# Two MoE blocks on one core: small broadcasts later at the opening, router products ahead of the norm's root, selections in fewer instructions

## The reference, cut to what matters

```python
h2 = rms_norm(x, norm2_gain[l]) * (1.0 + sc2) + sh2          # block 1
logits = (xf @ w_router + b_router)                           # 256 x 32
top_vals, top_idx = lax.top_k(logits, TOP_K)                  # top 4, softmax over them
# each of 32 experts: 1024 -> 2048, clipped SwiGLU, 1024 -> 1024
h2 = rms_norm_2(x, norm_ffn_g[l])                             # block 2
g_logits = hf @ w_rg + b_rg; e_logits = hf @ w_re + b_re      # 4 groups, 8 experts in each
# top 1 group, top 2 in it; 32 experts 1024 -> 2 x 256 -> 1024
```

## Time and profile before

| | us |
|---|---|
| median of 3 runs | 1674.42 (1673.65 to 1681.63) |
| profiled execution, whole time | 1677.89 |
| its span in the trace | 1676.10 |
| PE busy | 1496.8 (89%) |
| DVE busy | 645.1 (38%) |
| ACT busy | 326.2 (19%) |
| POOL busy | 11.9 (1%) |

### The profile page before, as it was taken

The page is one execution under the profiler, slowest core; times in us unless marked ns, Lnnn a source line. Parts: engine busy times, 40 slices in busy tenths (PEclk is TensorE's granted clock), DMA queues, the critical chain, the costliest instruction groups (busy, mean ns, idle before and its releaser), DMA issues.

```text
span 1676.1 us, 21107 instructions
## 1 busy us (share of the span) xinstructions
PE 1496.8 (89%) x8666; PEld 768.8 (46%) x8666; DVE 645.1 (38%) x1086; ACT 326.2 (19%) x374; POOL 11.9 (1%) x24
## 2 busy tenths in 40 slices
PE   3998999999989999898999989899889899997677
PEld 1776976333323333232333323233249898654343
DVE  2878576132313222231322223132257586431211
ACT  2444332110101011010101101010033454111110
POOL 1000000000000000000000000000000000000000
PEclk9999999999999999999999999999989899998989
DMA  9956255799999999999999999999955337599997
GB/s 349 355 226 252 101 179 214 323 428 430 427 429 427 430 427 430 427 430 427 429 428 429 428 429 428 429 428 429 425 195 200 105 147 279 239 415 422 422 422 296
DMA packets 73236, 592.31 MB, mean 353 GB/s; under 512 B 4946, under 2 KB 6056, under 8 KB 33252
## 3 DMA queue, kind: packets, MB, share of 16 engines
q1 hardware_dynamic: 71856, 588.27, 85.0%
q0 software_dynamic: 1088, 2.74, 0.7%
q10 hardware_dynamic: 244, 0.61, 0.1%
HBM read 590.55 MB, written 1.05 MB: 353 GB/s over the span
## 4 chain that ended last, share of the span: by engine, by line
DMA 50%; PE 37%; DVE 8%; ACT 2%; issue 2%; SPq 0%; DVEq 0%; ACTq 0%
DMA ring<-in_w_up 41%; PE PS L488 33%; DMA ring<-in_w_up_e 4%; DMA ring<-in_w_down_e 3%; PE PS L626 2%; DMA arena<-in_w_in 2%; DVE ring_r L330 1%; PE PS L648 1%; ACT ring_r L325 1%; DVE arena_r L330 0%; DVE arena L1758 0%; DVE arena L1999 0%; ACT arena L983 0%; PE PS L1198 0%; PE PS L578 0%
## 5 line engine op out<-in xcount | busy, mean ns | idle before, releaser
L488 PE MATMUL PS<-ring,arena 128*64 128x512 f32 x3072 | 686.4, 597 | 65.0 <-DMA ring<-in_w_up 57.6
L488 PEld LDWEIGHTS PS<-ring,arena 128*64 128x64 f32 x3072 | 212.6, 137 | 501.6 <-issue 385.5
L488 PE MATMUL PS<-arena 64*128 64x512 f32 (+12 forms) x1176 | 217.4, 448 | 13.3 <-DVE arena L2050 4.5
L703 DVE TENSOR_SCALAR arena<-PS 128x512 f32<-128x512 f32 x32 | 22.1, 692 | 514.4 <-PE PS L488 514.4
L488 PE MATMUL PS<-ring_r 128*128 128x256 f32 (+1 forms) x608 | 187.8, 313 | 0.0
L488 PEld LDWEIGHTS PS<-arena 128*64 128x64 f32 (+6 forms) x1176 | 105.6, 170 | 122.9 <-issue 107.9
L468 ACT ACTIVATE arena<-arena 128x512 f32<-128x512 f32 x32 | 20.2, 630 | 725.8 <-DVE arena L703 725.8
L488 PE MATMUL PS<-hT_r,ring_r 128*128 128x256 f32 x800 | 153.0, 288 | 1.7 <-DVE ring_r L330 1.7
L330 DVE TENSOR_TENSOR ring_r<-ring,ring_r 128x2048 fp32r<-128x2048 f32 x51 | 116.4, 2291 | 52.0 <-ACT ring_r L325 51.1
L488 PEld LDWEIGHTS PS<-hT_r,ring_r 128*128 128x128 f32 x800 | 129.1, 195 | 4.4 <-DVE ring_r L330 2.1
L325 ACT ACTIVATE ring_r<-ring 128x2048 fp32r<-128x2048 f32 x51 | 97.2, 1910 | 124.1 <-PE PS L488 113.5
(11 more groups left out here) (365 smaller groups left out, 1008.6 us busy)
## 6 DMA issues: line engine op xcount, KB each, us to landing
ring<-in_w_up SPq DMA_DIRECT2D x128, 2048.0 KB, 25.2
ring<-in_w_down SPq DMA_DIRECT2D x64, 2048.0 KB, 21.7
ring<-in_w_in SPq DMA_DIRECT2D x17, 2048.0 KB, 8.9
ring<-in_w_down_e SPq DMA_DIRECT2D x16, 2048.0 KB, 19.6
ring<-in_w_up_e SPq DMA_DIRECT2D x15, 2048.0 KB, 19.4
ring<-in_w_gate_e SPq DMA_DIRECT2D x14, 2048.0 KB, 20.9
ring<-in_w_ada SPq DMA_DIRECT2D x12, 2048.0 KB, 14.5
ring<-in_w_out SPq DMA_DIRECT2D x4, 2048.0 KB, 7.8
```

The lines of the kernel that those rows point to most:

```text
L488: return nc.tensor.matmul(o, w, m, start=first, stop=last)
L703: V.tensor_scalar(glu.rearrange("p (kk b q) -> p kk b q", kk=4, b=2), hu[:, :, :, :, 0], 7.0, None, ALU.min)\
```

## The change: what it does

**Opening.** In 0 is loaded as two halves; `consts` is cut: its first 136 columns stay on ACT's queue, the other 960 go on SP's queue behind in 0. The smalls wait on POOL until in 0 has landed, and behind a subtraction that POOL now does (the lower part of piece 0, DVE's before). `first_tokens` starts when the first four k-slices of `hT_up` are written. The n1 transposes stand ahead of ada 2 on PE.

**Routers.** n2: h without root and shift is transposed half by half and multiplied; the shift's share of the logits is a product of its own (added to `b_r1`); logits are scaled by `rs` afterwards. n4: the gain is multiplied before the root, and the logits scaled afterwards. Fewer `keep_warm` products stand between the steps. ACT does all of hT's copies in n2, and the first tile's in n4.

**Selections.** One DVE instruction with a broadcast operand replaces two (block 1) or eight (block 2); the first gather waits for the first selection alone. `moe2_gather` signals each half, ACT copies each half.

```diff
@@ consts and first unit
-_const("inv_freq", ...)            # last
+_const("inv_freq", ...)            # behind "ident"
+NFIRST = CONST["inv_freq"][0] + CONST["inv_freq"][1]
+                if u == IN0:
+                    w = t["w_in"][0, :, IN_COLS[0][0]:IN_COLS[0][0] + 512].rearrange("(k p) n -> p k n", p=P)
+                    for half, name in ((0, "first_half"), (1, f"loaded{SLOT_OF[u]}")):
+                        sp.dma_start(slots[SLOT_OF[u]][:, 2048 * half:2048 * (half + 1)].rearrange("p (k n) -> p k n", n=512),
+                                     w[:, 4 * half:4 * half + 4, :]).then_inc(S(name), 16)
+                    sp.dma_start(consts[:, NFIRST:], t["consts"][:, NFIRST:]).then_inc(S("consts"), 16)
@@ POOL
+            pool.wait_ge(S("w_upper"), 1)
+            nc.gpsimd.tensor_tensor(PIECES[0][3], PIECES[0][2], upper(0), ALU.subtract).then_inc(S("first_lower"), 1)
+            wait(pool, loaded(IN0))
             small_load(sm("hg_gain"), bc(t["hg_norm_gain"][0]), "smalls")
@@ PE, opening
-            ada(2)
             transpose_h(pe, "n1")
+            ada(2)
             ada(3)
...
-            pe.wait_ge(S("hT_V"), 1)
-            pe.wait_ge(S("hT_A"), 1)
             first_tokens()
@@ PE, router 1
-            keep_warm(7, 7)
-            transpose_h(pe, "n2")
-            router_mm(pe, "n2", sm("w_r1").rearrange("p (k n) -> p k n", k=KD), NE)
-            keep_warm(4, 7)
+            transpose_half(pe, 0)
+            pe.wait_ge(S("gain_free"), 1)
+            for k in range(KD):
+                last = mm(PS[:, 6, 480:512], sm("shiftT")[:, k:k + 1].broadcast_to([P, P]), w_r1[:, k, :], k == 0, k == KD - 1)
+            last.then_inc(S("logits"), 1)
+            keep_warm(1, 7)
+            transpose_half(pe, 1)
+            pe.wait_ge(S("hT_A"), 2)
+            for i in range(TT):
+                router_mm(w_r1, NE, i, range(4))
+            for i in range(TT):
+                pe.wait_ge(S("hT_A"), 3 + i)
+                last = router_mm(w_r1, NE, i, range(4, KD))
+            last.then_inc(S("logits"), 1)
+            keep_warm(2, 7)
             positions_mm(pe, "n2")
@@ DVE, logits of both routers
+            def logits(n, name, ne):
+                v.wait_ge(S("logits"), n)
+                for i in range(TT):
+                    last = STT(out=LG[:, i, 0:ne], in0=PS[:, 4 + i, 0:ne], scalar=sm("rs")[:, i:i + 1], in1=sm(name),
+                               op0=ALU.mult, op1=ALU.add)
+                L(last)
@@ DVE, selection of block 2
-        def moe2_select(X, e0, iota):
-            for i in range(TT):
-                for j in range(4):
-                    c = i * P + j * CAP2
-                    col = bass.ds(e0 + j, 1)
-                    V.tensor_scalar(selS2[:, c:c + CAP2], iota, SL[:, i, col], None, ALU.is_equal)
-                    last = V.tensor_scalar(selW2[:, c:c + CAP2], iota, SL[:, i, col], G[:, i, col], ALU.is_equal, ALU.mult)
+        def moe2_select(v, X, g, e0, iota):
+            cols_ = bass.ds(e0, 4)
+            for i in range(TT):
+                tile = selS2[:, i * P:(i + 1) * P].rearrange("p (j s) -> p j s", j=4)
+                last = V.tensor_tensor(tile, bc_mid(iota, 4), bc_last(SL[:, i, cols_], CAP2), ALU.is_equal)
+            last.then_inc(S(f"{X}_sel"), 1)
+            v.wait_ge(S(f"{X}_sel"), 2 * g + 1)
+            for i in range(TT):
+                s_, w_ = (a[:, i * P:(i + 1) * P].rearrange("p (j s) -> p j s", j=4) for a in (selS2, selW2))
+                last = V.tensor_tensor(w_, s_, bc_last(G[:, i, cols_], CAP2), ALU.mult)
             last.then_inc(S(f"{X}_sel"), 1)
```

More of the change, by code:

```diff
@@ L448, in rms_sums @@
                             .then_inc(S("squares"), 1)
+                if i == 0 and between:
+                    between()
             act.wait_ge(S("mean_square"), k)
             nc.scalar.sqrt(sm("rs"), sm("ss")[:, 0:2]).then_inc(S("rms"), 1)
[L452 to L455, removed]
         def moe1_act_gather(act, X, g):
@@ L472, in moe2_act_gather @@
         def moe2_act_gather(act, X, g):
-            act.wait_ge(S(f"{X}_gath_done"), g + 1)
-            nc.scalar.activation(xg2, PS[:, 0:2, :], ACT.Copy).then_inc(S(f"{X}_xg"), 1)
+            for b in range(2):
+                act.wait_ge(S(f"{X}_gath_done"), 2 * g + b + 1)
+                nc.scalar.activation(xg2[:, 512 * b:512 * (b + 1)], PS[:, b, :], ACT.Copy).then_inc(S(f"{X}_xg"), 1)
         def moe2_act(act, X, it, last):
@@ L503, in transpose_h, with transpose_half, router_mm @@
                 last.then_inc(S("h_transposed"), 1)
-        def router_mm(pe, n, w, ne):
+        def transpose_half(pe, half):
+            pe.wait_ge(S("h"), 3 + half)
             for i in range(TT):
[L507 to L510, removed]
+                for k in range(4):
+                    c = (4 * half + k) * P
+                    last = nc.tensor.transpose(PS[:, 2 * half + i, k * P:(k + 1) * P], h[:, i, c:c + P], ident)
+            last.then_inc(S("h_transposed"), 1)
+        def router_mm(w, ne, i, ks):
+            for k in ks:
+                last = mm(PS[:, 4 + i, 0:ne], hT[:, k, i * P:(i + 1) * P], w[:, k, :], k == 0, k == KD - 1)
+            return last
         def positions_mm(pe, n):
@@ L1230, in _ @@
             ada(6)
+            pe.wait_ge(S("consts"), 16)
             qk = at(A1MAP, "qk").rearrange("p (t b w) -> p t b w", t=TT, w=P)
@@ L1349, in _ @@
                 spread(1, j)
+            o = aux_bank()
+            for c in range(4):
+                last = nc.tensor.transpose(o[:, c * P:(c + 1) * P], modrow[:, 1, c * P:(c + 1) * P], ident)
+            last.then_inc(S("aux_done"), 1)
             pe.wait_ge(S("hg_out"), 1)
@@ L2131, in _ @@
                 sig(V.memset(sm("ang"), 0.0), "x_ready")
-            rms("n4", 12)
-            v.wait_ge(S("ffn_gain"), 16)
-            gained("n4", at(A2MAP, "gain"))
-            hT_copy_dve("n4")
-            v.wait_ge(S("logits"), 2)
-            L(TV(LG[:, :, :], logits[:, :, 0:36], bc_mid(sm("b_r2"), TT), ALU.add))
+                v.wait_ge(S("ffn_gain"), 16)
+                for i in range(TT):
+                    last = TV(h[:, i, :].rearrange("p (k q) -> p q k", k=KD)[:, 64 * j:64 * (j + 1), :],
+                              x[:, i, c].rearrange("p (q k) -> p q k", k=KD),
+                              at(A2MAP, "gain")[:, c].rearrange("p (q k) -> p q k", k=KD), ALU.mult)
+                if j:
+                    sig(last, "h")
+            rms("n4", 12)
+            v.wait_ge(S("h_transposed"), 8)
+            sig(CP(hT[:, :, P:256], PS[:, 2:4, :].rearrange("p b (k n) -> p (b k) n", n=P)), "hT_V")
+            for i in range(TT):
+                last = TS(h[:, i, :], h[:, i, :], sm("rs")[:, i:i + 1], None, ALU.mult)
+            L(last)
+            logits(3, "b_r2", 36)
             L(CP(GL[:, :, 0:4], LG[:, :, 0:4]))
```

248 lines of the change are left out of this document (131 added, 117 removed).

## The result

| | before | changed |
|---|---|---|
| median | 1674.66 (4 runs) | 1655.26 (1653.48 to 1660.88, 4 runs) |
| ratio | | 0.9881, 95% interval 0.9844 to 0.9918 |
| a second series | 1672.93 (14 runs) | 1656.35 (6 runs), ratio 0.9899 (0.9874 to 0.9923) |
| profiled execution, span | 1676.10 | 1651.9 |
| PE, DVE, ACT, POOL busy | 1496.8, 645.1, 326.2, 11.9 | 1476.2, 623.9, 328.7, 16.3 |

The kernel is 19.4 us (1.2%) faster at the median, 16.6 in the second series; forecast were 17.6. The two profiled spans differ by 24.2. I go through the changed kernel in order of time; start and duration in us, then what.

The account below looks back on a forecast made before the run. Bound by waits for loads in the opening, PE then loads in block 1's experts, DMA in block 2's; 6.7 - 0.6 + 6.1 - 1.0 + 7.9 - 1.5 = 17.6 us, from 1674.42 to 1656.8, range 1648 to 1667.

Parts of the forecast that it names:

- Opening, 6.7: Up to `split_lower(5)`: in 3 lands at 62.3 and the split starts at 64.2 instead of 70.90, 6.7 us gained.
- PE's gain: Opening: PE starts `first_tokens` near 32.3 instead of 44.29; 11 to 13 us gained on PE by round 0's end.
- Shift's share, -0.6: Ahead of round 10: four PE transposes and a DVE copy at a bank hand-over cost 0.6 us.
- Router 1, 6.1 - 1.0: Block 1's router: logits 3.8, positions 1.3, first gather 1.0 earlier, sum 6.1; half clock costs 1.0.
- Router 2, 7.9 - 1.5: Block 2's router: logits 3.6, positions' wait 0.79, selections 2.4, gather in halves 1.1, sum 7.9; half clock costs 1.5.
- Cold gathers: Rival: both gathers at half clock, 3.4 at each place where 2.5 in all is charged; 1661, chance 0.15.
- the 4 us that were to show the forecast wrong: Sign against the forecast: stretches around both gathers stand at 0.50 clock for over 4 us.
- Opening gives nothing: Rival: DMA engines were full to 57.3, only order changes; the opening gains 1 instead of 6.7; 1662.5, chance 0.12.
- slower: Rival: POOL's subtraction holds `first_tokens` and smalls, costing nothing up to 9.5 us, one for one after; chance 0.03.
- Signs: Router 1's logits some 10 us earlier, its gather some 12; block 2's gate products near 1443 to 1446 instead of 1461.4.

Follow-up runs that it names:

- e6: Changed kernel with DVE's copy of round 0 ahead of `split_lower(3)`, while DVE waits for in 2; its one execution took 1658.90.
- e3: Changed kernel with the first subtraction on DVE instead of POOL, which issues the smalls once in 0 has landed; 1658.44, ratio 0.9907.
- e5: Changed kernel with shift transposes and DVE's copy behind the last modulation rows, and b_up and b_down loads issued ahead of the gain's; 1671.75.
- E1: Kernel before with only the opening's part of the change, routers and selections as before; 1668.73 against 1674.39, ratio 0.9964.
- e9: Changed kernel with shift transposes in bank 7 ahead of the rows, b_up loaded earlier, round 0 copied earlier, more `keep_warm` products; median 1657.49, ratio 0.989.
- e4: Changed kernel with four instead of two `keep_warm` products between logits and positions in router 1, five instead of two in router 2; 1658.81, ratio 0.9912.
- e11: Changed kernel with the old selections, two DVE instructions in block 1 and sixteen in block 2; its one execution took 1659.97.
- e12: The same program as e9, run for a second profile; the execution took 1654.41.

## Why the prediction was right, step by step

The forecast of 17.6 holds, and so does its mechanism in each part. That the sum comes so close is in part luck: the opening was over-sized by 2.0 and router 1 under-sized by 2.9.

- **Opening, 6.7.** 7.4 at `split_lower(5)`, right in size. The step's reason was in part wrong: "in 3 lands at 62.3, ACT's split, 64.2" was to set the moment. In 3 did come early (60.77), and with it out of the way DVE's chain behind in 2 was the next limit (e6), 0.8 later, one that the prediction did not name. What it called PE's gain (44.29 to about 32.3) came, 33.94, and e3 shows that 2.5 us of it more or less are nothing.
- **Shift's share, -0.6.** 0.8 (5.6 to 4.8 earlier across the hand-over, and e5's rows). E1, which has no shift transposes, begins router 1 0.6 earlier than the changed kernel.
- **What it left out.** Between 174 and 235 us 7.2 became 4.1: besides the 0.8, 1.5 between 175 and 211, where PE took 35.62 for the 264 products for which it had taken 34.11 (the clock was at half from 176 to 180), and 0.7 at ACT's wait for b_up (13.76 instead of 12.19), which e5 and e9 took back. So the term "6.7 - 0.6" was 4.1 at the router: over-sized by 2.0.
- **Router 1, 6.1 - 1.0.** 4.9 at the first expert, where 5.1 stood, and 7.95 by the third. Logits 4.15 (3.8 forecast), DVE's wait for positions gone as forecast; of the last 1.0 only 0.4 came to pass, since PE was held by a `keep_warm` product at half clock. The term that was mis-sized is the clock's. It was charged at the gather alone, 1.0, and the gather stage did lose 1.46 against e4. But the kernel before paid too, and later: its first expert had half clock from 312 to 320, in dense work, and took 3.1 more than the changed kernel's. Counted against that, the clock gave about 1.6 in these two profiles where it was to cost 1.0.
- **Router 2, 7.9 - 1.5.** 6.7, where 6.4 stood; clock 1.41 by e4 (1.5 forecast), so 8.1 without it. Logits 3.3 (3.6 forecast), from logits to gather 2.3 in spite of the clock (0.8 and 2.4 forecast; the selections alone are 1.9 by e11), the gather in halves 1.1 as forecast.
- **Sum.** 4.1 + 7.95 + 6.7 = 18.7 where 17.6 stood; the measured 19.4 (intervals 13.7 to 26.1 and 12.9 to 21.1 in the two series) holds both. The forecast's closeness to the median, 1.6 us, is better than the measurement can tell.
- **Rivals.** "Cold gathers" was half true: the stretches came (0.57 over 4 us, 0.72 over 12), at router 2 in two parts, 1421 to 1426 and 1428 to 1433, together longer than the 4 us that were to show the forecast wrong. By e4 they cost the two stages 2.9 instead of the 2.5 charged, not 6.8, and only the 1.4 of router 2 came through. "Opening gives nothing" and "slower" fell: POOL's 4.53 against a bound of 9.5.
- **Signs.** The logits of router 1 came 8.2 earlier and its gather 9.7, where some 10 and 12 were named: what the opening lost on its way. The gate products came at 1435.73, earlier than the 1443 to 1446 named, mostly by the clock in block 2's projections and in the first expert.

What stays open: why the clock of unchanged stretches differs from execution to execution. The profiles show where, not why. The earlier logits and the block 2 gather in halves are read from rows alone; no run takes them back one by one.

## What to carry to other kernels

When a load that was late is moved early, look for the engine that has queued work behind the load before it; that work is the next limit, and the gain is the distance to it. A bank or buffer handed over between two engines is freed by an instruction in the other's queue: before work is moved to a quiet place, look up what stands ahead of that instruction (0.8 us were to be saved, 10.58 were lost). And filler products in an idle gap ahead of dense work are worth what is left of them further on: here 1.4 us at router 2 and 0.1 at router 1, where the half clock only moved into the first expert. They must end with the arrival of the awaited result; those behind the last dependent step hold the engine. So read a gain at the first row behind which both traces run alike, not at the end of the stage that was changed.

## What the runs showed that I had not expected

While the smalls are in flight the DMA engines are full but move fewer bytes, wherever the smalls stand: 273 GB/s from 45 to 50 us against 421 from 20 to 25 in the changed kernel, and 336 against 422 from 10 to 20 before, where they were loaded first. And two executions of one program differ by 6 us (e9, e12), where the granted clock differs.

```profile
45.00:50.00 5.00, 5.00 (x32) 2.78 (x31) 0.00 (x0) 0.00 (x0) 0.00 (x0) 1.00 1.07 273
20.00:25.00 5.00, 2.48 (x22) 0.74 (x19) 2.26 (x13) 0.32 (x2) 0.00 (x0) 1.00 1.01 421
```
